# A decoder trunk in float32 pairs: feed-forward norms by a matrix of equal weights

## What is computed

```python
def rmsnorm(x, g):
    x32 = x.astype(jnp.float32)
    y = x32 * lax.rsqrt(jnp.mean(x32 * x32, axis=-1, keepdims=True) + EPS)
    return (y * g.astype(jnp.float32)).astype(x.dtype)

def conv_glu_ffn(xn, w_up, conv_w, conv_b, w_down):
    u = causal_dwconv3(xn @ w_up, conv_w) + conv_b
    gate, up = jnp.split(u, 2, axis=-1)
    return (jax.nn.silu(gate) * up) @ w_down
```

## Time and profile before

| | us |
|---|---|
| median of 3 runs (1114.18 to 1114.37) | 1114.19 |
| the profiled execution, its own time | 1114.31 |
| its span, first to last instruction | 1112.4 |
| TensorE busy | 1106.1 (99%) |
| VectorE busy | 584.6 (53%) |
| ScalarE busy | 499.3 (45%) |
| GpSimd busy | 462.4 (42%) |

### The profile page before, as it was taken

One profiled execution on the slowest core, in us unless ns is written; L12 is line 12 of the kernel. 1 busy time (PEld: TensorE's weight loads), 2 busy tenths in 40 slices (PEclk: granted clock), 3 DMA queues, 4 the chain that ended last, 5 costly groups with the idle time before them and its releaser, 6 DMA issues.

```text
span 1112.4 us, 15737 instructions
## 1 busy us (share of the span) xinstructions
PE 1106.1 (99%) x5252; PEld 943.6 (85%) x5252; DVE 584.6 (53%) x1070; ACT 499.3 (45%) x807; POOL 462.4 (42%) x221
## 2 busy tenths in 40 slices
PE   9999999999999999999999999999999999999998
PEld 7788888888888888889999999888888888888887
DVE  6785755444454521125688888877644454540000
ACT  5333434443444423233777778644543444442120
POOL 4454544444435354543223233144544435344442
PEclk9999999999999999999999999999999999999999
DMA  8232313323232233333222333132323232224331
GB/s 269 77 115 87 122 64 107 103 86 113 80 109 85 64 105 103 93 94 118 76 77 76 102 99 95 49 105 85 123 85 113 80 108 94 78 67 116 90 108 71
DMA packets 47125, 108.19 MB, mean 97 GB/s; under 512 B 4272, under 2 KB 19632, under 8 KB 47088
## 3 DMA queue, kind: packets, MB, share of 16 engines
q1 hardware_dynamic: 44752, 103.46, 29.6%
q10 hardware_dynamic: 2336, 4.24, 1.6%
HBM read 105.54 MB, written 2.15 MB: 97 GB/s over the span
## 4 chain that ended last, share of the span: by engine, by line
PE 97%; DVE 2%; ACT 0%; DMA 0%; issue 0%; SPq 0%; ACTq 0%; DVEq 0%
PE bank L1189 17%; PE bank L1187 17%; PE bank L1188 17%; PE spt L1188 8%; PE spt L1187 8%; PE spt L1189 8%; PE bank L1370 4%; PE bank L1372 4%; PE bank L1371 4%; PE obank L1473 2%; PE spt L1455 1%; PE spt L1444 1%; PE spt L1445 1%; PE bank L1430 1%; PE bank L1250 1%; PE bank L1253 0%
## 5 line engine op out<-in xcount | busy, mean ns | idle before, releaser
L449 POOL TENSOR_TENSOR wl<-raw,wh 128x1024 fp32r<-128x1024 f32 (+2 forms) x214 | 458.2, 2146 | 624.9 <-ACT wh L484 624.8
L1187 PE MATMUL bank<-xh,wh 128*128 128x512 f32 x800 | 311.7, 390 | 0.0
L1189 PE MATMUL bank<-xh,wl 128*128 128x512 f32 x800 | 311.3, 389 | 0.0
L1188 PE MATMUL bank<-xl,wh 128*128 128x512 f32 x800 | 311.2, 389 | 0.0
L484 ACT ACTIVATE wh<-raw 128x1024 fp32r<-128x1024 f32 (+2 forms) x214 | 202.0, 946 | 152.3 <-PE spt L1189 138.3
L966 DVE TENSOR_TENSOR work<-bank,rstd 128x512 f32<-128x512 f32 x88 | 60.6, 691 | 225.6 <-PE bank L1189 223.6
L1187 PEld LDWEIGHTS bank<-xh,wh 128*128 128x128 f32 x800 | 150.2, 188 | 31.9 <-issue 0.9
L1188 PEld LDWEIGHTS bank<-xl,wh 128*128 128x128 f32 x800 | 150.2, 188 | 31.3
L1189 PEld LDWEIGHTS bank<-xh,wl 128*128 128x128 f32 x800 | 150.2, 188 | 30.9
L1187 PE MATMUL spt<-bh,wh 128*128 128x512 f32 x408 | 158.8, 389 | 0.0
L1188 PE MATMUL spt<-bl,wh 128*128 128x512 f32 x408 | 158.7, 389 | 0.0
(11 more groups left out here) (154 smaller groups left out, 1197.2 us busy)
## 6 DMA issues: line engine op xcount, KB each, us to landing
raw<-w_up SPq DMA_DIRECT2D x88, 512.0 KB, 3.3
raw<-w_down SPq DMA_DIRECT2D x32, 384.0 KB, 3.1
raw<-w_qkv SPq DMA_DIRECT2D x32, 384.0 KB, 3.3
raw<-w_down SPq DMA_DIRECT2D x32, 320.0 KB, 2.9
raw<-w_in SPq DMA_DIRECT2D x14, 512.0 KB, 3.7
raw<-w_out SPq DMA_DIRECT2D x8, 512.0 KB, 3.3
work<-bias_rows ACTq DMA_DIRECT2D x16, 256.0 KB, 4.1
raw<-w_o SPq DMA_DIRECT2D x8, 512.0 KB, 3.5
```

Of the source, the lines that this page charges most:

```text
L449: nc.gpsimd.tensor_tensor(wl[s][:, 0:n], raw[s][:, 0:n], plain(wh[s][:, 0:n]), ALU.subtract).then_inc(s_lo, 1)
L1187: mm(dst, wh[s][:, w], hi, start=first, stop=False)
L1188: mm(dst, wh[s][:, w], lo, start=False, stop=False)
L1189: return mm(dst, wl[s][:, w], hi, start=False, stop=last)
```

## The change

For norms 1 and 3, `acc` is split like everything else: ScalarE rounds it to `acc_h`, VectorE subtracts to `acc_l` (`rest_of_squares`). Both lie in the last tile of `bh` and `bl`. TensorE multiplies both by `ones`, a 128x128 matrix whose entries are all 1/1024 (`wide_stats`, two 128x512 matmuls): every partition of `nbank` then holds the mean of squares of all 512 positions. VectorE computes the reciprocal root on 128x512 (`wide_rsqrt`), straight into `rstd`. The spreading and ScalarE's copy go. The pair stands before tile 6 of `first_two` in layer 0 and after 2 of the 8 products of up unit 2 in layer 1. ScalarE rounds units up+3, up+4 and up+5 before its first bias pass. Norms 0 and 2 stay as they are; the waits on `s_rn` count one less.

```diff
+        ones = sb("ones", [P, P], F32R)
...
+        wide = tiles([SEQ] * 4)
+        acc_h, acc_l = bh[:, FT - 1, :], bl[:, FT - 1, :]
...
@@ ScalarE @@
+            nc.scalar.activation(ones[:], spread(col(C_ONE), [[0, P]]), ACT.Copy).then_inc(s_ones, 1)
...
                 prep(norm, KT - 1)
+                act.wait_ge(s_acc, (norm + 1) * (KT + 1))
+                nc.scalar.activation(acc_h, acc[:], ACT.Copy).then_inc(s_acc_h, 1)
...
-                def hidden(i, j, first=False):
+                def hidden(i, j, first=False, early=False):
...
-                    ahead(up, i, 2 * j)
                     if first:
-                        keep_rstd(keep)
+                        for n in range(3):
+                            ahead(up, 0, n)
+                    elif not early:
+                        ahead(up, i, 2 * j)
                     act.wait_ge(s_z, f * 2 + 1)
...
-                    ahead(up, i, 2 * j + 1)
+                    if not first:
+                        ahead(up, i, 2 * j + 1)
                     act.wait_ge(s_z, f * 2 + 2)
...
-                hidden(0, 1)
+                hidden(0, 1, early=True)
@@ VectorE @@
+            def rest_of_squares(norm):
+                dve.wait_ge(s_acc_h, norm // 2 + 1)
+                nc.vector.tensor_tensor(acc_l, acc[:], plain(acc_h), ALU.subtract).then_inc(s_acc_l, 1)
+
+            def wide_rsqrt(norm):
+                dve.wait_ge(s_ms, norm + 1)
+                v, half, t, y = wide
+                g = y.bitcast(I32)
+                link(nc.vector.tensor_scalar(v, nbank, EPS, None, ALU.add))
+                link(nc.vector.tensor_scalar(g, v.bitcast(I32), -0.5, MAGIC, ALU.mult, ALU.add))
+                link(nc.vector.tensor_scalar(half, v, -0.5, None, ALU.mult))
+                for n in range(3):
+                    link(nc.vector.tensor_tensor(t, y, y, ALU.mult))
+                    link(nc.vector.tensor_tensor(t, t, half, ALU.mult))
+                    if n < 2:
+                        link(nc.vector.scalar_tensor_tensor(y, t, 1.5, y, ALU.add, ALU.mult))
+                nc.vector.scalar_tensor_tensor(rstd[:], t, 1.5, y, ALU.add, ALU.mult).then_inc(s_rstd, 1)
...
                 prep(phase + 1, KT - 1)
-                norm_rsqrt(phase + 1)
+                rest_of_squares(phase + 1)
+                wide_rsqrt(phase + 1)
@@ TensorE @@
+            def wide_stats(norm):
+                pe.wait_ge(s_ones, 1)
+                pe.wait_ge(s_acc_l, norm // 2 + 1)
+                mm(nbank, ones[:], acc_h, start=True, stop=False)
+                mm(nbank, ones[:], acc_l, start=False, stop=True).then_inc(s_ms, 1)
...
-                    if not late and k == 4:
-                        norm_stats(norm)
-                    if not late and k == KT - 1:
-                        norm_spread(norm)
+                    if not late and k == 6:
+                        wide_stats(norm)
...
                 if late:
-                    norm_stats(norm)
                     unit_ready(up + 2)
-                    up_part(2, 0, 5)
-                    norm_spread(norm)
-                    up_part(2, 5, KT).then_inc(s_unit, 1)
+                    up_part(2, 0, 2)
+                    wide_stats(norm)
+                    up_part(2, 2, KT).then_inc(s_unit, 1)
```

More of the change, by code:

```diff
@@ L236, in trunk @@
         s_bc = sem("s_bc")
+        s_ones = sem("s_ones")
+        s_acc_h = sem("s_acc_h")
+        s_acc_l = sem("s_acc_l")
         s_rstd = sem("s_rstd")
@@ L581, in residual @@
                 prep(norm, KT - 1)
+                act.wait_ge(s_acc, (norm + 1) * (KT + 1))
+                nc.scalar.activation(acc_h, acc[:], ACT.Copy).then_inc(s_acc_h, 1)
             def ffn(layer, up, down):
-                keep = layer + 2
-                def hidden(i, j, first=False):
+                def hidden(i, j, first=False, early=False):
                     f = i * 2 + (layer * FT + j)
                     c = C_FFN + layer * FT * 8 + j * 8
-                    ahead(up, i, 2 * j)
                     if first:
-                        keep_rstd(keep)
+                        for n in range(3):
+                            ahead(up, 0, n)
+                    elif not early:
+                        ahead(up, i, 2 * j)
                     act.wait_ge(s_z, f * 2 + 1)
@@ L654, in evacuate @@
                 if pair == 0:
-                    act.wait_ge(s_rn, 3)
+                    act.wait_ge(s_rn, 2)
                 nc.scalar.activation(v_heads(pair, t, lo=False), v_part(b), ACT.Copy,
@@ L1134, in _ @@
                     nc.vector.memset(plain(bl[half(1 - h), KREST[parity][h], :]), 0.0)
-            dve.wait_ge(s_rn, 3)
+            dve.wait_ge(s_rn, 2)
             for p in range(LAST):
```

## The result

Runs of both kernels taken in turn on one chip:

| | before, us | changed, us |
|---|---|---|
| median of 6 runs each | 1114.14 | 1118.28 |
| lowest to highest | 1114.00 to 1114.37 | 1117.40 to 1119.38 |
| the profiled execution, its own time | 1114.31 | 1117.84 |
| its span | 1112.4 | 1116.0 |
| mean granted clock of the profiled execution | 1.000 | 0.998 |

The account below looks back on a forecast made before the run. TensorE, busy 99% of the span, was taken to bound the kernel. Removed TensorE work -1.92, layer 1's wait +3.9 and layer 0's +0.5 gave +2.5 us on 1114.2: 1116.7 us, range 1112.6 to 1118.5.

Parts of the forecast that it names:

- TensorE's own time: In norms 1 and 3, two wide matmuls replace sums and spreading: 0.96 us gained per norm, 1.92 in all.
- VectorE's series: The reciprocal root's twelve VectorE operations on 512 columns, instead of 4, take 8.27 us undisturbed.
- The lock: VectorE operations with both ends in SBUF wait for running GpSimd subtractions, twice per layer; 4.3 us in layer 0.
- Layer 1's wait: TensorE wants bank 0 at 770.68, before VectorE's first evacuation at 774.3, and waits 3.9 us.
- Layer 0's wait: TensorE wants bank 0 at 164.96, before VectorE's first evacuation at 165.25, and waits 0.5 us.
- the trace's row so far speaks for a wait this short passing unpunished: The clock stayed 1.00 for 3.3 us after the last matmul, so layer 1's 3.9 us should not lower it.
- that rival: TensorE's clock falls in layer 1's wait, half rate costing 1.9 to 3.7 us: 1118.6 to 1120.4; chance 0.08.
- a granted clock below 1: One of the listed signs that would show the forecast wrong: TensorE's granted clock reading below 1.
- own range: 1115.7 to 1118.2 us, from bounds on tensor_scalar prices (-0.4 to +0.8) and the pair (up to +0.98).
- The first rival: GpSimd does not hold up VectorE's series; layer 1 waits 0.3 us: 1112.6; chance 0.18 including a partial version.
- The second wait: TensorE also waits for up+7's weights, 1.7 us late after two more lock turns: 1118.4 us; chance 0.04.

Follow-up runs that it names:

- e3: Changed kernel with the edits of e1 and e2 together; 1112.35 us, ratio 0.9981 to the kernel before.
- e5: Changed kernel with ScalarE's old order of roundings, one unit before and one behind the first bias pass; 1119.60 us, ratio 1.0048.
- e1: Changed kernel with two tiles of VectorE's wide series in idle PSUM banks and the Newton product in another order; 1113.11 us, ratio 0.9990.
- e2: Changed kernel with layer 1's pair of wide matmuls right behind first_two, six matmuls earlier; 1118.49 us, ratio 1.0033.
- e4: Changed kernel with ScalarE's rounding of up+5 moved behind the first bias pass; 1114.62 us, ratio 1.0000.
- e6: e3 with six linked memsets before VectorE's series in layer 1, making TensorE wait 3.18 us; 1117.00 us, ratio 1.0023.
- e10: e3 with five linked memsets before VectorE's series in layer 1, making TensorE wait 2.53 us; 1116.04 us, ratio 1.0013.
- e8: e3 with twelve linked memsets before VectorE's series in layer 1, making TensorE wait 7.13 us; 1122.01 us, ratio 1.0072.
- e7: e3 with seven linked memsets before VectorE's series in layer 1, making TensorE wait 3.84 us; 1117.60 us, ratio 1.0032.

## Why the prediction came out as it did

**TensorE's own time: right.** The forecast said 0.96 per norm, e3 measured 0.91. The pair steps 0.227 each like its neighbours; what it disturbs around it makes the rest.

**VectorE's series: right.** 8.27 us was forecast and 8.15 is what it takes undisturbed (e5). The PSUM read is 0.69 as taken. The two SBUF tensor_scalars take 0.43, not the 0.49 of the earlier trace rows.

**The lock: right, and it decides.** Two turns in each layer, as the order of ScalarE's roundings had told. They cost 3.55 and 4.16 us (the forecast had 773.2 - 769.6 = 3.6 and 4.3). e1 takes the lock away and leaves the order on every engine, e2 adds a turn, e4 removes one, and each moves the wait by what the rows give. The turns followed from two stretched rows in another part of the kernel. The Trainium skill (SBUF — State Buffer, "Who interferes with whom") says that VectorE and GpSimd share a port pair by an exclusive lock, taken by operations with two SBUF inputs or in a two-port mode, and left alone by one with a single SBUF input outside that mode. The trace agrees: 1.91, 2.50 and 2.77 us for the first two kinds, 0.69 and 0.70 in e1.

**Layer 1's wait: right.** 3.9 was forecast and 3.60 came. rstd stood at 772.30; shifted by the 0.77 us that the stage began earlier, the forecast's 773.2 is 772.4.

**Layer 0's wait: too high by half.** 0.5 against 0.27. A quarter of a microsecond decides nothing.

**The step that failed: "the trace's row so far speaks for a wait this short passing unpunished".** That the clock falls in the wait had a chance of 0.08; it fell in all six runs, and made 1.7 us of the profiled execution's loss, nearly the whole distance from the forecast. The price in that rival (1.9, from the earlier trace rows) was close; the chance was wrong, and with it the number. Without the fall the sum would have been -1.83 + 3.60 + 0.27 + 0.1 = +2.1, beside the forecast's +2.5. The error lies in what was made of the earlier trace rows: one stretch without matmuls, at the end of one execution, at a clock of 1.00. It is shorter than the wait of 3.9 that it was to speak for, and it is one draw. The same tail in the changed kernel's trace reads less, and so it does in e1, e2, e6 and e10, while it reads 1.00 in the seven other traces:
```profile
1112.72:1116.00 3.28, 0.00 (x0) 0.00 (x0) 0.69 (x1) 0.00 (x0) 0.00 (x0) 0.86 0.21 80
```
There the fall comes 2.7 us after the start of the last matmul (1112.33 to 1115.07). So a pause of this length can go either way, and with 3.60 us of wait the fall came in all six runs. The Trainium skill (TensorE: Matmul & The Clock Gate, "What's actually happening") says that an idle array goes back to half rate and needs activity to leave it. The measurement bears it out (0.50 inside e8's wait), and its rule deserved the larger chance, for want of any row in which TensorE had paused for 2 to 4 us in mid-stream. The prediction had named "a granted clock below 1" as a sign of being wrong, and this sign came.

**The bounds of the forecast: one sum is wrong.** Its "own range", 1115.7 to 1118.2, doesn't follow from the bounds given with it: 1116.7 - 0.4 is 1116.3, and 1116.7 + 0.8 + 0.98 is 1118.5. Nothing else rests on it.

**The first rival, "the lock does not bite": fell**, though its arithmetic was good. It said 1112.6 if nothing held the series up. e1, where nothing does, measured 1113.11, its wait of 0.59 being 0.3 longer since its tensor_scalars run at 0.70.

**The second wait: did not come.** TensorE has no other wait in layer 1.

## What to carry to other kernels

When small operations become wide ones on VectorE, look first at what GpSimd does in those microseconds; a long linked series is best run with one operand of each operation in PSUM, and only then is an earlier start worth its full length. Where TensorE bounds the kernel, a wait can cost more than its own length (here from somewhere between 1.9 and 2.5 us on), since matmuls run at half rate behind it. That the granted clock reads 1.00 over one idle stretch of one execution promises nothing for another, nor for the matmuls right behind it: look at several executions, and at the stretch after a restart.

## What the runs showed that was not expected

- By the mean clock, the fall is a matter of chance between two lengths of wait: never at 0.6, 1.5 and 1.9 us (32 runs), in 6 of 10 at 2.5 and 8 of 10 at 3.2, in every run from 3.3 to 7.1 (28 runs with the changed kernel's six).
- The fall shows 2.9 to 4.0 us after the start of the last matmul before the wait. With a short wait that is behind the restart (0.2 us in the changed kernel, 0.9 in e10), with a long one inside it (e5, e7, e8). The first costs some 1.7 us, the second 2.7 to 2.9, half of the low time behind the restart.
- A 128x512 tensor_scalar from SBUF to SBUF takes 0.43 us, also on int32 views; with an operand in PSUM 0.70. A 128x512 memset takes 0.48 and, linked to the next by a semaphore, steps 0.66, where a linked tensor_tensor of 0.69 steps 0.73: the link costs 0.17 in one case and 0.03 in the other. Why was not tried.
